# Attention of a hybrid layer: bias and row maximum in one VectorE pass in PSUM, scores in pieces of 512 and 128 columns, the fifth turned chunk in a bank of its own job

## What is computed

```python
# neighbourhood attention, per head, q of 64 latent columns by 8 rows
s_loc = einsum(q, k_local) * HEAD_DIM ** -0.5 + bias      # bias from rpb
s_loc = where(valid, s_loc, NEG_INF)                       # window of 16 columns
s_ctx = einsum(q, k_context) * HEAD_DIM ** -0.5
p = softmax(concatenate([s_loc, s_ctx]))
o = p_loc @ v_local + p_ctx @ v_context
# differential attention, per head
p = softmax(einsum(q_i, k_i) * DF_QK ** -0.5)              # i = 0, 1
o = (p[0] - lam * p[1]) @ v
```

## Time and profile before

| | |
|---|---|
| median of three runs | 3142.87 us |
| the profiled execution, its own time | 3147.49 us |
| its span | 3145.8 us |
| PE busy, share of the span | 2800.2 us, 89% |
| DVE busy | 1816.3 us, 58% |
| ACT busy | 1309.7 us, 42% |
| POOL busy | 305.2 us, 10% |
| mean granted PE clock | 0.935 |
| latent attention, layer 0 | 540.48 to about 748.9 us |
| latent attention, layer 1 | 1867.39 to about 2080 us |

### The profile page before, as it was taken

How to read it: one execution, slowest core, us unless ns; L and a number is a source line. 1 busy time by engine, 2 the same in 40 slices (tenths; PEclk the granted TensorE clock), 3 DMA queues, 4 the chain that set the end, 5 groups by cost and what they waited for, 6 DMA issues and landing times.

```text
span 3145.8 us, 50930 instructions
## 1 busy us (share of the span) xinstructions
PE 2800.2 (89%) x21300; PEld 2467.9 (78%) x21300; DVE 1816.3 (58%) x2770; ACT 1309.7 (42%) x1870; POOL 305.2 (10%) x295
## 2 busy tenths in 40 slices
PE   6998887997699999879988889987799999999992
PEld 5996675676699899769966666776698989999992
DVE  2144555666622222342545556666588888888886
ACT  2123222444222122131332224442577777777773
POOL 0001212001200000100012210010100000000003
PEclk7999997999899999979999979998899999999996
DMA  5234211000121212241122110003799999999993
GB/s 213 72 128 147 96 69 60 1 1 6 55 75 66 89 68 71 84 148 68 55 97 108 57 60 1 1 14 122 282 373 353 366 361 360 371 353 378 353 367 122
DMA packets 76514, 477.39 MB, mean 152 GB/s; under 512 B 10224, under 2 KB 13808, under 8 KB 26864
## 3 DMA queue, kind: packets, MB, share of 16 engines
q1 hardware_dynamic: 52672, 316.84, 27.0%
q0 software_dynamic: 23616, 157.30, 13.4%
HBM read 455.49 MB, written 27.53 MB: 154 GB/s over the span
## 4 chain that ended last, share of the span: by engine, by line
PE 74%; DVE 12%; ACT 5%; issue 4%; DMA 3%; POOL 1%; SPq 0%; DVEq 0%; ACTq 0%
PE psum L1299 15%; PE psum L1198 10%; PE psum L850 8%; PE psum L1321 8%; PE psum L1228 4%; PE psum L1159 4%; PE psum L876 3%; PE psum L1106 3%; DMA ring<-in_ada 2%; PE psum L985 2%; PE psum L1064 2%; ACT stage_rounded L1597 2%; PE psum L973 2%; PE psum L1091 1%; PE psum L996 1%
## 5 line engine op out<-in xcount | busy, mean ns | idle before, releaser
L1299 PE MATMUL psum<-stage_rounded 128*128 128x256 f32 x3728 | 571.8, 287 | 10.9 <-DVE ring_rounded L1675 4.2
L1299 PEld LDWEIGHTS psum<-stage_rounded 128*128 128x128 f32 x3728 | 512.9, 191 | 27.8 <-DVE ring_rounded L1675 11.8
L1675 DVE TENSOR_TENSOR ring_rounded<-ring,stage_rounded 128x2048 fp32r<-128x2048 f32 (+1 forms) x145 | 319.4, 2217 | 2.4 <-ACT stage_rounded L1597 2.4
L1675 DVE TENSOR_TENSOR stage_rounded<-stage,stage_rounded 128x2048 fp32r<-128x2048 f32 (+1 forms) x144 | 318.1, 2224 | 0.0
L1597 ACT CAST stage_rounded<-ring 128x2048 fp32r<-128x2048 f32 (+1 forms) x145 | 269.3, 1863 | 43.5 <-PE psum L1321 28.8
L1597 ACT CAST stage_rounded<-stage 128x2048 fp32r<-128x2048 f32 (+1 forms) x144 | 268.5, 1869 | 42.9 <-PE psum L1321 28.1
L1321 PE MATMUL psum<-stage_rounded 128*128 128x512 f32 x940 | 252.1, 394 | 0.1
L1491 ACT ACTIVATE stage<-psum,arena 128x640 f32<-128x640 f32 (+1 forms) x180 | 126.5, 706 | 232.4 <-DVE arena L2017 232.4
L1299 PE MATMUL psum<-ring_rounded,stage_rounded 128*128 128x256 f32 x760 | 215.4, 283 | 0.0
L1321 PEld LDWEIGHTS psum<-stage_rounded 128*128 128x128 f32 x940 | 175.1, 188 | 43.0 <-DVE stage_rounded L1675 3.8
L1106 PEld LDWEIGHTS psum<-stage 128*128 128x128 f32 x1008 | 136.9, 207 | 66.9 <-issue 35.8
(11 more groups left out here) (321 smaller groups left out, 5857.7 us busy)
## 6 DMA issues: line engine op xcount, KB each, us to landing
ring<-in_ada SPq DMA_DIRECT2D x48, 1024.0 KB, 5.2
ring<-in_moe_gu SPq DMA_DIRECT2D x48, 1024.0 KB, 7.0
ring<-in_moe_gu POOLq DMA_DIRECT2D x47, 1024.0 KB, 7.0
stage<-in_moe_gu SPq DMA_DIRECT2D x46, 1024.0 KB, 6.7
stage<-in_moe_gu POOLq DMA_DIRECT2D x46, 1024.0 KB, 6.2
ring<-in_unit SPq DMA_DIRECT2D x22, 1024.0 KB, 4.8
stage<-in_moe_down SPq DMA_DIRECT2D x22, 1024.0 KB, 7.8
stage<-in_moe_down POOLq DMA_DIRECT2D x22, 1024.0 KB, 8.1
```

Of the source, the lines that this page charges most:

```text
L1299: mm = pe.matmul(bank(h % 2, 0, 2 * P), r32(x[:, cols]), w[:, k, :], start=(k == 0 and m == 0), stop=(k == KD - 1 and m == 2))
L1675: v.tensor_tensor(r32(w), w, high(M_HIGH[q % M_HI][:, 0:n]), ALU.subtract).then_inc(v_mlo, 1)
```

## The change

The bias is no longer added by PE. For na jobs the query scale is negative, so PSUM holds minus the scores; the table `tab` holds mask minus bias with a mask of +1e30; DVE first reduces the 128 context columns to their minimum in a new column `nbc`, waits for itself, and then one `tensor_tensor_reduce` adds the table to the 512 latent columns, writes them back into the same PSUM bank and takes the minimum with `nbc` as its start. The minimum is the negated maximum, and ACT's exponential gets `scale=-1.0`.

To make this possible an item's scores lie as 512 latent columns (the whole bank `b`) and 128 context columns (start of bank `b + 1`), for df jobs too. Values are read in the matching order (`(s + 1) % n`). The fifth turned chunk moves from bank 7 to columns 128 to 255 of bank `b + 1` of the job's own item. The fifth transpose no longer waits for `v_o`; instead `mix_values` waits for it, and the 128-column score matmul waits for `v_pt` (the copy `move_last` of the job that used the bank three items ago) where that bank held a turned chunk.

```diff
@@ scores
-                        elif kind == "na":
-                            pe.wait_ge(s_ctx_na, 32 * (l + 1))
-                            pe.wait_ge(g_tab, H_NA * l + h + 1)
-                            j0 = 7 - 2 * (t - 1) - 1
-                            near_bias = tab[:, h, j0:j0 + ROWS, :].rearrange("p r k -> p (r k)")
-                            for g in range(2):
-                                pe.matmul(bank(b + g, 0, HALF), q, FT[rows, ki, g * HALF:(g + 1) * HALF],
-                                          start=True, stop=False, tile_position=pos)
-                            pe.matmul(bank(b, P, HALF), ident, near_bias[:, 0:HALF - P], start=False, stop=True)
-                            mm = pe.matmul(bank(b + 1, 0, HALF), ident, near_bias[:, HALF - P:4 * P], start=False, stop=True)
                         else:
-                            pe.wait_ge(s_ctx_df, 32 * (l + 1))
-                            for g in range(2):
-                                mm = pe.matmul(bank(b + g, 0, HALF), q, FT[rows, ki, g * HALF:(g + 1) * HALF],
-                                               start=True, stop=True, tile_position=pos)
+                            pe.wait_ge(s_ctx_na if kind == "na" else s_ctx_df, 32 * (l + 1))
+
+                            pe.matmul(bank(b), q, FT[rows, ki, P:TOK], start=True, stop=True, tile_position=pos)
+                            k = job_of(it - 3)
+                            if jobs[k][0] and chunk_item(k) == it - 3:
+
+                                pe.wait_ge(v_pt, N_FIVE * l + five_before[k + 1])
+                            mm = pe.matmul(bank(b + 1, 0, P), q, FT[rows, ki, 0:P], start=True, stop=True, tile_position=pos)
@@ turn_probs
-                        if s == 4:
-
-                            pe.wait_ge(v_o, JOBS * l + j)
-                        dst = bank(6, s * P, (s + 1) * P) if s < 4 else bank(7, 0, P)
+                        dst = bank(6, s * P, (s + 1) * P) if s < 4 else last_chunk(j)
@@ mix_values
-                    elif j:
+                    if j:
 
                         pe.wait_ge(v_o, JOBS * l + j)
@@ exps
-                            src = psum[:, b * BANK:(b + 2) * BANK].rearrange("p (g t) -> p g t", g=2)[:, :, 0:HALF]
-                            dst = prob[s].rearrange("p (g t) -> p g t", g=2)
-                        act.activation(dst, src, ACT.Exp, bias=nb[:, s:s + 1], accum_out=sm[:, s:s + 1]).then_inc(a_exp, 1)
+                        w = TOK if t else P
+
+                        act.activation(prob[s][:, 0:w], psum[:, b * BANK:b * BANK + w], ACT.Exp, bias=nb[:, s:s + 1],
+                                       scale=-1.0 if kind == "na" else 1.0, accum_out=sm[:, s:s + 1]).then_inc(a_exp, 1)
@@ maxima
-                        src = psum[:, b * BANK:(b + 2) * BANK].rearrange("p (g t) -> p g t", g=2)[:, :, 0:HALF] if t else bank(b, 0, P)
-                        v.tensor_reduce(nb[:, s:s + 1], src, AX.XY if t else AX.X, ALU.max, negate=True).then_inc(v_nb, 1)
+                        if kind == "df":
+                            v.tensor_reduce(nb[:, s:s + 1], psum[:, b * BANK:b * BANK + (TOK if t else P)], AX.X, ALU.max,
+                                            negate=True).then_inc(v_nb, 1)
+                        elif t == 0:
+                            v.tensor_reduce(nb[:, s:s + 1], bank(b, 0, P), AX.X, ALU.min).then_inc(v_nb, 1)
+                        else:
+
+                            link(v.tensor_reduce(nbc[:, s:s + 1], bank(b + 1, 0, P), AX.X, ALU.min))
+                            v.wait_ge(g_tab, H_NA * l + h + 1)
+                            j0 = 7 - 2 * (t - 1) - 1
+                            v.tensor_tensor_reduce(bank(b), bank(b), tab[:, h, j0:j0 + ROWS, :].rearrange("p r k -> p (r k)"), 1.0,
+                                                   nbc[:, s:s + 1], ALU.add, ALU.min, nb[:, s:s + 1]).then_inc(v_nb, 1)
```

More of the change, by code:

```diff
@@ L154, in constants @@
     cs = np.clip(q - WIN_C // 2, 0, GRID_W - WIN_C)
-    c[:, C_BIAS:C_BIAS + GRID_W] = np.where((k >= cs) & (k < cs + WIN_C), 0, NEG)
+    c[:, C_BIAS:C_BIAS + GRID_W] = np.where((k >= cs) & (k < cs + WIN_C), 0, -NEG)
     c[:, C_IOTA:C_IOTA + EXPERTS] = np.arange(EXPERTS)
@@ L314, in build @@
         (z, zr, za, sp, gg, beta, eg, tl, cd, egb) = parts(misc, *[TILES * 8] * 10)
+        nbc = misc[:, 704:704 + SLOTS]
         gct, alog, mx, nb, sm, rc, cc, lamw, lam, st6, mv, rstd, subw, ssq, lampr, wts = parts(
@@ L603, in query_scale, with chunk_item, last_chunk @@
         def query_scale(i):
-            return HD ** -0.5 if i < 3 else DFQ ** -0.5 if 12 <= i < 15 else 1.0
+            return -HD ** -0.5 if i < 3 else DFQ ** -0.5 if 12 <= i < 15 else 1.0
         def job_of(it):
             return max(n for n in range(JOBS) if first_item[n] <= it)
+        def chunk_item(j):
+            return first_item[j] + (jobs[j][1] == "df")
+        def last_chunk(j):
+            return bank(2 * (chunk_item(j) % 3) + 1, P, 2 * P)
         five_before = [sum(j[0] > 0 for j in jobs[:n]) for n in range(len(jobs) + 1)]
@@ L1106, in mix_values @@
                         mm = pe.matmul(bank(7, 256, 256 + P), probT[j % 2][:, s * P:(s + 1) * P],
-                                       VT[:, s, v_at:v_at + P], start=(s == 0), stop=(s == n - 1))
+                                       VT[:, (s + 1) % n, v_at:v_at + P], start=(s == 0), stop=(s == n - 1))
                     mm.then_inc(s_pv, 1)
@@ L1485, in exps @@
                             act.wait_ge(s_pt, JOBS * l + job_of(it - SLOTS) + 1)
-                        if t == 0:
-                            src, dst = bank(b, 0, P), prob[s][:, 0:P]
-                        else:
-                            src = psum[:, b * BANK:(b + 2) * BANK].rearrange("p (g t) -> p g t", g=2)[:, :, 0:HALF]
-                            dst = prob[s].rearrange("p (g t) -> p g t", g=2)
-                        act.activation(dst, src, ACT.Exp, bias=nb[:, s:s + 1], accum_out=sm[:, s:s + 1]).then_inc(a_exp, 1)
+                        w = TOK if t else P
+                        act.activation(prob[s][:, 0:w], psum[:, b * BANK:b * BANK + w], ACT.Exp, bias=nb[:, s:s + 1],
+                                       scale=-1.0 if kind == "na" else 1.0, accum_out=sm[:, s:s + 1]).then_inc(a_exp, 1)
                 def move_probs(j):
@@ L2042, in move_last @@
                         v.wait_ge(s_pv, JOBS * l + j - 1)
-                    v.tensor_copy(probT[j % 2][:, 4 * P:TOK], bank(7, 0, P)).then_inc(v_pt, 1)
+                    v.tensor_copy(probT[j % 2][:, 4 * P:TOK], last_chunk(j)).then_inc(v_pt, 1)
                 def outputs(j):
@@ L2313, in _ @@
                 for h in range(H_NA):
-                    pool.tensor_tensor(tab[:, h], tab[:, h], win_mask.unsqueeze(1).broadcast_to([P, NA_J, GRID_W]), ALU.add).then_inc(g_tab, 1)
+                    pool.tensor_tensor(tab[:, h], win_mask.unsqueeze(1).broadcast_to([P, NA_J, GRID_W]), tab[:, h], ALU.subtract).then_inc(g_tab, 1)
                 for c in range(OUT_LOADS):
```

## The result

The changed kernel takes 3113.1 us, the median of four runs (3110.3 to 3115.4), against 3142.6 us for four of the kernel before. The ratio is 0.9896, with a 95% interval of 0.9882 to 0.9909: 1% faster, 29.5 us. The profiled execution has a span of 3112.1 us (3145.8 before), 33.7 us less.

The account below looks back on a forecast made before the run. PE's queue was taken to bound undisturbed latent steps, DVE the tile ends. Savings of 24 us in 27 steps, 0 in 15 and 6 at the starts, 30 us, gave 3113 us, range 3103 to 3122, chance 0.46.

Parts of the forecast that it names:

- 27 steps: Latent attention steps away from tile ends: 7.59 us falls to 6.7, 0.9 saved each, 24 us in all.
- the starts: Half-clock start of each layer's latent segment: 3 us saved a layer, 6 us in all.
- The bound: Undisturbed latent steps: PE's own queue bounds them at 7.59 us; after the change PE alone would need 6.27.
- na scores: PE's na score matmuls with bias: 2.24 us falls to 1.26, saving 0.98 us.
- turns: PE's two turns of a step: 0.80 and 0.94 us become 0.70 each, saving 0.34 us.
- The pass on DVE: 512-column addition with minimum 0.69 us, taking out its result 0.20; whole na maximum 1.21 us, 0.39 more than before.
- The rule of the Trainium skill: Two-tensor DVE operations with accumulator run at half throughput for non-bf16 SBUF sources; if it applied, the pass takes 1.1 us.
- The chains: Latent step after the change: 6.49 us through DVE and ACT, 6.62 through PE; with small waits 6.7 a step.
- The tile ends: 15 latent steps bound by DVE's square sums: no change expected, between -0.5 and +0.5 us each.
- PE alone as the bound: Rival for the latent steps: result read hidden, waits fall between, 48 us saved, 3095 us; chance 0.18.
- The slow pass: Rival: DVE's 512-column pass takes up to 1.38 us; 3140 us, or 3127 at half; chance 0.20 for 3122 to 3136.
- The falling clock: Rival: PE's waits of about 0.4 us a step lower its clock, 37 us lost, 3174 us; chance 0.07.

Follow-up runs that it names:

- e6: Changed kernel with the 128-column minimum of each latent na item made twice: 3123.8 us, ratio 0.9940 to the kernel before.
- e10: Changed kernel with only DVE's normalizing of tiles 0 to 3 moved behind the last latent job, ACT's output norms left: 3117.1 us, ratio 0.9895.
- e7: Changed kernel with ACT's output norms and DVE's normalizing of tiles 0 to 3 moved behind the last latent job, square sums left: 3089.5 us, ratio 0.9835.
- e11: Kernel before the change with output norms and normalizing of tiles 0 to 3 behind the last latent job, square sums left: 3133.0 us, ratio 0.9949.
- e3: Kernel before the change with square sums, output norms and normalizing of tiles 0 to 3 behind the last latent job: 3137.3 us, ratio 0.9977.
- e4: Changed kernel with square sums, output norms and normalizing of tiles 0 to 3 behind the last latent job: 3085.7 us, ratio 0.9814.
- e5: Changed kernel with ACT's copy for a df job put in front of the na exponential: 3125.5 us, ratio 0.9944.
- e8: Changed kernel with DVE's square sums and normalizing put behind the copy of the fifth chunk: 3120.5 us, ratio 0.9931.
- e9: Changed kernel with output norms and normalizing behind the last latent job and square sums behind the fifth chunk's copy: 3083.5 us, ratio 0.9785.
- e2: Changed kernel with the bias added on PE again and the maximum in one reduction; layout and chunk's place kept: 3153.9 us, ratio 1.0025.
- e12: Changed kernel with the fifth chunk back in bank 7, and output norms and normalizing behind the last latent job: 3101.4 us, ratio 0.9846.

## Why the prediction was right

The time was forecast as 3113 us and is 3113.1. That is closer than the terms were, and part of it is luck. The sum had 24 us for 27 steps, 0 for 15 and 6 for the starts. Counted on the same steps (one of 8.09 us, at the first tile end of layer 1, was among the 27) the profiled executions show 26.7 gained, 5.2 lost and 5.1 gained, 26.6 us in all. Another 7.0 came from places that the sum did not have: 2.3 in the tails and 4.7 outside the latent attention.

**The bound.** PE's queue held the steps, in the stretch as read. PE alone was put at 6.27 us a step and every other step takes 6.27 to 6.29. The single terms: na scores 1.26 against 1.27 measured, turns 0.70 against 0.64 each, and the mixing behind the na scores, kept at 1.11, takes 1.22; these misses cancel.

**The pass on DVE.** Addition 0.69, result 0.20: in the trace the next work starts 0.68 us after the start of the pass, together with the read. The na maximum occupies DVE for 1.00 us, not 1.21, and holds ACT up for 1.17. The rule of the Trainium skill ("Vector Engine (DVE) Microarchitecture Reference", section 7) on half throughput did not apply, with one source in PSUM: 512 columns took 0.76 us, near the 0.69 of the plain addition and not the 1.1 that was estimated from the rule.

**The chains.** Put at 6.49 (DVE and ACT) and 6.62 (through PE), with 6.7 chosen for the step; measured 6.48 on average. The mechanism was right in its parts, ACT's exponential ahead of PE's copy and all. From the end of the df combination to the df mixing it took 2.50 us (640.14 to 642.64), not 2.91, of which the hidden read is a part. But the chain does not hold every step, as forecast: the loop closes over two steps (e6), and every other one is PE's queue alone.

**The tile ends.** "I set 0 for these 15 steps, between -0.5 and +0.5 each": this is the term that was wrong in its mechanism. The 16 steps lost 7.8 us, the 15 of the prediction 5.2, which is within its bounds, but by a path that it did not have. I had followed DVE's sums and the new wait, and had not followed ACT's output norm, whose 3 us lie in front of the copy that PE needs. The trace of the kernel before already had that wait at five tile ends (2.63 us at 562.76), and the clock of 0.70 that I took for the mark of DVE's sums stands behind it. PE's longer queue had covered a part of it; e10 against e7 shows that it is now the largest part of a tile end (37.9 of 48.9 us in the 42 steps), and the half clock that follows makes it larger. Without the loads the square sums cost 1 us more than before (e7 against e11), probably as the steps have less slack; no run isolates that.

**The starts.** 5.1 us where 6 stood, and 2.3 in the tails that were not in the sum.

**The rivals.** PE alone as the bound (3095) failed on the wait of 0.33 us in every other step, and on the tile ends. The slow pass did not happen. The falling clock did not happen where it was feared: 1.00 in undisturbed stretches. It did at the tile ends, which is the half of that rival I should have priced.

## What to carry to other kernels

When the bound engine gets shorter by a sixth, go through everything that stands in front of its suppliers' small copies, the rare work too: two table loads on ACT that had been partly covered became the dearest thing at the tile ends, and moving them away with the normalizing (e7) was worth 19 us more on top of the change. A gain by step should be measured once with the rare work moved aside (e3 and e4); it showed 52 us where the kernel got 29. Moving one wait out of a nearly closed chain (e5, e8) is worth nothing or less; the version to keep is e9, 3083.5 us, ratio 0.9785, though the traces do not show why it is ahead of e7.

## What the runs showed of the hardware

- A VectorE pass over 128x512 fp32 that reads PSUM and SBUF, writes back into PSUM and keeps a minimum has a row of 0.76 us, and the next work follows 0.68 us after its start; the plain addition into SBUF has 0.69. Writing to PSUM and the running minimum are at most 0.07 us.
- The instruction that takes the result out of VectorE has a row of 0.14 us, and the next instruction on VectorE starts together with it.
- On TensorE two more changes between matmuls of 64 and of 128 rows went with 0.39 us more at full clock (e2 against the earlier trace rows), about 0.2 us each as an estimate; no run changes that alone. Scores split as 512 + 128 or as 320 + 320 columns take the same time (1.27 us each).
- A wait between two of the four df score matmuls did not break the overlap of the two row groups: the scores take 1.30 us, 1.28 before.
- The same wait of TensorE, 1.09 us for DVE's copy, was followed by full clock in one place and by half clock in another: in e12 the ten passes behind it take 1.35 us at 601.91 (granted clock 1.00) and 2.47 us at 1902.09 (0.50).
